# A weights' ring moved by 128 bytes in a one-core kernel of two transformer blocks

## What is computed

```
first block (16 meta tokens ahead of the 256):
    h = h + hybrid_mixer(rmsnorm(h), w_in, ..., w_out)    # attention with forget gates | short convolution
    h = h + (silu(n @ w_gate) * (n @ w_up)) @ w_down       # n = rmsnorm(h), 2048 -> 5632 -> 2048
    x = rmsnorm(h)[16:]
second block (256 context tokens beside x):
    shifts, scales, gates = silu(c) @ w_mod + b_mod        # and the same for c_ctx
    x = x + gate1 * (mix(rmsnorm(x) * (1 + scale1) + shift1, ctx) @ w_out)
    x = x + gate2 * conv_ffn(rmsnorm(x) * (1 + scale2) + shift2)    # 2048 -> 2 x 5632 -> 2048
    return rmsnorm(x)
```

## Time and profile before

| | us |
|---|---|
| median of 3 runs | 2354.27 |
| the three runs | 2351.6, 2354.27, 2383.33 |
| profiled execution, own time | 2354.1 |
| its span, first to last instruction | 2352.1 |
| TensorE matmul busy | 2342.0 |
| VectorE busy | 1663.2 |
| ScalarE busy | 1123.4 |
| mean granted clock of TensorE | 1.000 |

### The profile page before, as it was taken

How to read it: one execution, slowest core, us unless ns; L and a number is a source line. 1 busy time by engine, 2 the same in 40 slices (tenths; PEclk the granted TensorE clock), 3 DMA queues, 4 the chain that set the end, 5 groups by cost and what they waited for, 6 DMA issues and landing times.

```text
span 2352.1 us, 49789 instructions
## 1 busy us (share of the span) xinstructions
PE 2342.0 (100%) x19292; PEld 2279.5 (97%) x19292; DVE 1663.2 (71%) x2501; ACT 1123.4 (48%) x1500; POOL 0.2 (0%) x4
## 2 busy tenths in 40 slices
PE   9999999999999999999999999999999999999998
PEld 9998899999999999999988989799999999999998
DVE  6676678788877878888887755456666566655675
ACT  6354445544445554445632332455555355544554
POOL 0000000000000000000000000000000000000000
PEclk9999999999999999999999999999999999999999
DMA  7875566588778887787657722054565665666664
GB/s 284 285 272 195 188 233 233 198 285 303 273 255 283 280 285 240 264 290 270 224 200 258 258 80 93 22 175 166 192 196 194 194 191 187 199 193 191 197 192 143
DMA packets 141889, 509.19 MB, mean 216 GB/s; under 512 B 15824, under 2 KB 17360, under 8 KB 141392
## 3 DMA queue, kind: packets, MB, share of 16 engines
q1 hardware_dynamic: 141776, 507.60, 64.1%
HBM read 505.44 MB, written 2.10 MB: 216 GB/s over the span
## 4 chain that ended last, share of the span: by engine, by line
PE 99%; DVE 0%; DMA 0%; ACT 0%; SPq 0%; issue 0%; ACTq 0%
PE ps L1175 30%; PE ps L1177 30%; PE ps L1176 30%; PE ps L1517 1%; PE ps L1203 1%; PE ps L1205 1%; PE ps L1204 1%; PE ps L1535 1%; PE ps L1349 1%; PE ps L1526 0%; PE ps L1330 0%; PE ps L1374 0%; PE ps L1583 0%; PE ps L1355 0%; DMA raw<-in_stream 0%; PE ps L1331 0%
## 5 line engine op out<-in xcount | busy, mean ns | idle before, releaser
L1717 DVE TENSOR_TENSOR lo<-raw,hi 128x1024 fp32r<-128x1024 f32 x753 | 918.4, 1222 | 489.4 <-ACT hi L584 485.1
L584 ACT ACTIVATE hi<-raw 128x1024 fp32r<-128x1024 f32 x753 | 797.0, 1061 | 969.3 <-PE ps L1177 864.0
L1175 PE MATMUL ps<-hs,hi 128*128 128x256 f32 (+1 forms) x3056 | 860.7, 282 | 0.4 <-DVE hs L2526 0.3
L1176 PE MATMUL ps<-hs,hi 128*128 128x256 f32 (+1 forms) x3056 | 859.8, 281 | 0.0
L1177 PE MATMUL ps<-hs,lo 128*128 128x256 f32 (+1 forms) x3056 | 859.8, 281 | 0.0
L1176 PEld LDWEIGHTS ps<-hs,hi 128*128 128x128 f32 x3056 | 576.2, 189 | 5.0
L1175 PEld LDWEIGHTS ps<-hs,hi 128*128 128x128 f32 x3056 | 573.7, 188 | 6.2 <-DVE hs L2526 0.8
L1177 PEld LDWEIGHTS ps<-hs,lo 128*128 128x128 f32 x3056 | 573.7, 188 | 5.1
L1175 PE MATMUL ps<-hid,hi 128*128 128x256 f32 x1408 | 388.7, 276 | 0.0
L1176 PE MATMUL ps<-hid,hi 128*128 128x256 f32 x1408 | 388.6, 276 | 0.0
L1177 PE MATMUL ps<-hid,lo 128*128 128x256 f32 x1408 | 388.6, 276 | 0.0
(11 more groups left out here) (323 smaller groups left out, 2537.2 us busy)
## 6 DMA issues: line engine op xcount, KB each, us to landing
raw<-in_stream SPq DMA_DIRECT2D x753, 512.0 KB, 4.3
wm<-in_mod_stream SPq DMA_DIRECT2D x192, 512.0 KB, 4.8
out_tokens<-y_final SPq DMA_DIRECT2D x4, 512.0 KB, 3.7
h<-in_tokens SPq DMA_DIRECT2D x3, 544.0 KB, 8.7
cx<-in_ctx_tokens SPq DMA_DIRECT2D x6, 256.0 KB, 6.0
cbx<-in_c_rows SPq DMA_DIRECT2D x1, 1024.0 KB, 8.0
cbc<-in_c_rows SPq DMA_DIRECT2D x1, 1024.0 KB, 5.5
na<-in_na_bias SPq DMA_DIRECT2D x1, 1024.0 KB, 4.8
```

The costliest lines, as they stand in the source:

```text
L584: act.activation(hi[:, slot, :], raw[:, slot, :], ACT.Copy).then_inc(hi_done, 1)
L1175: pe.matmul(acc_, hi[:, slot, w], x_hi, start=kt == 0, stop=False)
L1176: pe.matmul(acc_, hi[:, slot, w], x_lo, start=False, stop=False)
L1717: dve.tensor_tensor(lo[:, slot, :], raw[:, slot, :], hi[:, slot, :].bitcast(F32), ALU.subtract)\
```

## The change

modx, the context's modulation vectors, is placed first instead of after mod. It takes 128 bytes, so raw, hi, lo, wm, cbx, h, cols, tabs and mod all begin 128 bytes higher, raw at 16640 = 65 x 256. From mp on every address is as before, the arena's too. No instruction, size, wait or order changes.

```diff
@@ -182,6 +182,7 @@
             top[0] += -(-4 * int(np.prod(shape[1:])) // 64) * 64
             return at(name, shape, dt, offset), offset
 
+        modx, _ = keep("modx", [P, CTX_TILES])
         raw, _ = keep("raw", [P, RING, CW])
         hi, _ = keep("hi", [P, RING, CW], F32R)
         lo, _ = keep("lo", [P, RING, CW], F32R)
@@ -192,7 +193,6 @@
         cols, _ = keep("cols", [P, N_COLS])
         tabs, _ = keep("tabs", [P, N_TABS])
         mod, _ = keep("mod", [P, MOD_TILES])
-        modx, _ = keep("modx", [P, CTX_TILES])
         mp, _ = keep("mp", [P, 3, 2])
         gm, _ = keep("gm", [P, 3, KT])
         pick, _ = keep("pick", [P, HEADS], F32R)
```

## The result

The changed kernel takes 2403.58 us (median of 4 runs, 2401.72 to 2403.91); the kernel before took 2353.82 us beside it. The medians are 49.8 us apart; the ratio is 1.0198, 95% interval 1.0138 to 1.0258, so slower by 1.4 to 2.6%. All ratios here take in the runs of an upper group of times, near 2380 us, that the kernel before has (one of its four runs here), and so lie a little under the quotients of the medians. The forecast was 2354 us and no change; what came is the rival "the new pairing has only the slow rhythm", priced at 2404.6 us.

A forecast was written before the change was run, and what follows sets the result against it. TensorE's own matmul pace was taken to bound the kernel. TensorE, VectorE, ScalarE and DMA were each put at 0, so 2354.1 + 0 gave 2354 us, with a range of 2320 to 2386 us that leaves 0.12 outside.

The forecast's parts named there:

- the new pairing has only the slow rhythm: Rival: operand reads collide on TensorE, every fast stretch of lines 1175 to 1177 slows, 50.5 us, 2404.6 us; chance 0.06.
- The bound: Whole kernel: TensorE busy 2342.0 of 2352.1 us, nothing feeding it late; only the matmuls' pace can change the time.
- 2382.6 us: Rival of one lock lost: ffn2, 717 us, falls into the slow rhythm, costing 28.5 us; chance 0.14.
- What decides between them is not the address of an operand: Lines 1175 to 1177: each stretch falls into one of two rhythms when entered, after an interruption, and keeps it.
- the value 0 that I took for the pace: TensorE's long stretches: no change of matmul pace from the new pairing, 0 us.
- The last sentence of the prediction: Long stretches: if all slow or all fast ones vanish at once, alignment sets the rhythm and the entry reading is wrong.
- The row that misled: Line 1203, moving operand 64 after stationary: 111.8 ns a matmul on hs, so this pairing too has the fast rhythm.
- The row that spoke against it: Line 1177 on xs1, 118 to 150 us: durations 276, 281 and 293 ns; change there taken as 0.
- The page on lines of 16 bytes: SBUF rule, penalty at each new 16-byte line: a 128-byte move could change no matmul; not taken as the whole story.
- VectorE, ScalarE and DMA at 0: Splits, modulation and ring loads: 0 each; 0.8 us if engine slack were gone, -0.6 to +0.6 us on the first load.
- The 3% by it: First ring load: estimate from the descriptor rule, 132 beats instead of 128 per 4096-byte row, 0.2 us; other loads hidden.

The follow-up runs named there:

- The square above: Four kernels, weights at 128 or 0, activations at 64 or 192 modulo 256: 128/64 2352.27 us, 128/192 2403.58, 0/64 2403.58, 0/192 2352.53.

## Why the prediction was wrong

- **The bound** was right: TensorE's own pace, no wait, no transfer. So was the observation that this pace takes few values and is redrawn at interruptions. The two groups of times are ffn2 in one rhythm or the other; 2382.6 us had been worked out for it, and the one profile taken in an upper-group run (ring at 0, arena at 192) shows just that.
- **The step that failed** is the sentence "What decides between them is not the address of an operand", with the value 0 that I took for the pace. It was drawn from up1a and up1b, which differ in rhythm at equal addresses. That shows only that at d = 192 the address leaves two rhythms open. It does not show that another d leaves them equally open, and none of the others does. At 64 every long stretch is slow, in three kernels and twelve runs (2401.7 to 2404.4 us), though short ones can still be fast; at 128 and 0 all are slower still, 118.3 and 119.8 ns in up1a. In the place of 0 the runs showed 4.4 ns a matmul over the fast stretches, 49 us. The last sentence of the prediction had named this outcome, all fast stretches gone at once, as the sign that this reading was wrong.
- **The row that misled** is line 1203. Its operands lie 64 apart in the same sense as those of lines 1175 to 1177 after the change, and it was fast. But its roles are swapped, which I noted against the slow rival's weakness and then gave too little weight. In the changed kernel the same line, at moving 0 and stationary 64, is still fast at 111.7 ns in the window, while the long stretches of lines 1175 to 1177 are slow. What the row showed, that a fast rhythm exists at a difference of 64, even holds for lines 1175 to 1177, in the two short stretches above. It did not show which rhythm the long stretches would take.
- **The row that spoke against it** was already there: line 1177 on xs1, 276 to 293 ns over starts that run through all multiples of 64. I used it to call that one stretch unchanged (rightly: 202 matmuls in 15 to 40 us before and 203 after) and not as evidence that the pairing sets the pace elsewhere.
- **The page on lines of 16 bytes**, of the Trainium skill ("SBUF — State Buffer", section "Specifications (TRN2)"), by whose rule a move by a multiple of 16 changes no matmul, is refuted here as a full account: moves by 32, 64 and 128 bytes all did. The Trainium skill also says, "TensorE: Matmul & The Clock Gate", section "Step-by-step: what each phase is for", that TensorE has two read ports and that loading the next weights takes nothing from the running matmul. The square above sits ill with it: the pace hangs on where the two operands lie to each other, and two reads that never meet would not seem to bring that about. That they meet in the memory is my inference; no run shows the reads themselves.
- **VectorE, ScalarE and DMA at 0** were right. Lines 1742 and 1740 have medians of 1219 and 1218 ns as in the earlier trace rows, and the median time to landing of the ring's loads is 4.2 us (4.3 before). The first load took 5.20 us of the chain after 5.74 before, but 5.77 in the other kernel with raw at 0, and 5.40 to 6.18 in those with raw at 128: scatter. The Trainium skill's rule on descriptors ("DMA: Bandwidth & Descriptors", "How a descriptor splits into AXI transactions") speaks of bytes fetched, and what moved here is the side that is written. The 3% by it is not to be seen in the queue that carries the ring's loads and the others. With raw at 0 its packets took 62.0% of 2399.9 us, 1488 us, and 1493 us in the other such kernel; with raw at 128 it is 61.7% of 2401.3 us, 1482 us, in the kernel with raw alone left there, 1508 us before the change, and 1479 to 1514 us over all of them.
- **The price of the slow rival** was right to a microsecond (2404.6 against 2403.58), in part by luck: the fast stretches lost 49.2 us, not 50.5, and the losses and gains elsewhere come to -1.4. Its chance, 0.06, was too low.

## What to carry to other kernels

Where the chain is nothing but matmuls whose weights are loaded anew each time, count matmuls per window before looking for waits: a spread of paces at one shape is time to be had. Then treat the two operands' start addresses, modulo 256 bytes, as a parameter of the kernel and try their difference rather than "aligned" addresses, each tensor by itself (here 128 bytes between hi and lo were worth 0.8%, 128 bytes ahead of both cost 2%). A small tensor moved in the list of allocations is enough to lose either, so the layout has to be written down and not left to follow from the order of declarations.

## What the hardware did that I had not expected

- The pace of a matmul of 256 fp32r columns beside a 128-column load follows the difference of the two starts modulo 256. In the long stretches it is 113.1 or 117.6 ns at 192, 117.5 at 64, 118.3 at 128 (119.6 in out2), 119.8 at 0; at 160 and 224 the kernels took 2415.75 and 2414.0 us. The same difference reached from different absolute starts gave the same time twice.
- At a difference of 192 there are two steady paces, kept for up to 717 us, and an interruption of under a microsecond can switch them. Which one a stretch takes can differ from run to run (ffn2). At 64 the same two exist, the fast one in stretches of 16 us and less only.
- A third of the loads at another start (lo at 0 under hi at 128) removes the slow one of the two from every long stretch.
- Open: why these paces, what lies between the steps of 32 bytes (not tried), and whether lo at 64 past a multiple of 256 (d = 0) would be better still (not tried).
